# A decoder of two blocks on one core: the filler products taken out of the norms and of the routing

## What is computed

```python
for l in range(DEPTH):                      # first block
    h = rms_norm(x, g_pre[l]) * (1.0 + scale) + shift
    ...                                     # projections, three attentions, gates -> y
    x = x + gate * rms_norm(y, g_post[l])
...
hn = rms_norm_2(h, norm_mix[0]); h = h + even_mixer(hn, ...)
h = h + swiglu(rms_norm_2(h, norm_ffn[0]), ...)
hn = rms_norm_2(h, norm_mix[1]); h = h + odd_mixer(hn, ...)
h = h + moe_swiglu(rms_norm_2(h, norm_ffn[1]), router, w1, w3, w2)
return rms_norm_2(h, norm_final)

logits = t @ router                         # inside moe_swiglu
top_vals, top_idx = lax.top_k(logits, 2)
top_w = softmax(top_vals)
```

## Time and profile before

| | |
|---|---|
| median of three timed runs | 1960.36 us (1958.73 to 1962.9) |
| the profiled execution | 1962.08 us |
| its span, first to last instruction | 1958.8 us |
| mean granted clock of TensorE | 0.988 |
| busy share of the span: PE, PE's weight loads, DVE, ACT | 98%, 80%, 61%, 49% |
| chain that ended last: PE, DMA, DVE, ACT | 62%, 2%, 1%, 1% |

### The profile page before, as it was taken

The page is one execution under the profiler, slowest core; times in us unless marked ns, Lnnn a source line. Parts: engine busy times, 40 slices in busy tenths (PEclk is TensorE's granted clock), DMA queues, the critical chain, the costliest instruction groups (busy, mean ns, idle before and its releaser), DMA issues.

```text
span 1958.8 us, 30650 instructions
## 1 busy us (share of the span) xinstructions
PE 1918.3 (98%) x12361; PEld 1570.0 (80%) x12361; DVE 1185.5 (61%) x1698; ACT 969.5 (49%) x1429; POOL 29.8 (2%) x29
## 2 busy tenths in 40 slices
PE   6999999999999999999999999999999999999998
PEld 4999899999899989999999736883588887368833
DVE  4767886565785776666663217951498884059611
ACT  3647753466863575443463206740476673057501
POOL 1000000000000120000000000000000000000000
PEclk7999999999999999999999999999999999999999
DMA  9985556465544542555455899999999999999997
GB/s 291 270 267 184 163 174 160 98 188 189 158 140 140 177 142 88 194 194 158 158 187 203 336 395 407 416 365 412 409 413 409 404 374 347 414 408 411 409 410 303
DMA packets 292565, 536.83 MB, mean 274 GB/s; under 512 B 67076, under 2 KB 198600, under 8 KB 278096
## 3 DMA queue, kind: packets, MB, share of 16 engines
q1 hardware_dynamic: 287968, 530.82, 75.4%
q10 hardware_dynamic: 3920, 3.69, 0.6%
q0 software_dynamic: 544, 0.43, 0.1%
HBM read 533.83 MB, written 1.07 MB: 273 GB/s over the span
## 4 chain that ended last, share of the span: by engine, by line
PE 62%; DMA 2%; DVE 1%; ACT 1%; issue 0%; SPq 0%; DVEq 0%
PE bank L803 14%; PE bank L805 14%; PE bank L804 13%; PE bank L1603 9%; PE bank L1630 4%; DMA pool<-in_od_exp_w 2%; PE bank L1411 1%; PE bank L1458 1%; PE bank L1487 1%; PE bank L1519 1%; PE bank L763 1%; PE bank L748 1%; PE bank L1616 0%; PE bank L788 0%; PE bank L779 0%
## 5 line engine op out<-in xcount | busy, mean ns | idle before, releaser
L3123 DVE TENSOR_TENSOR expert_lo<-pool,w_hi 128x2048 fp32r<-128x2048 f32 x168 | 376.9, 2287 | 46.6 <-ACT w_hi L2268 46.5
L2268 ACT ACTIVATE w_hi<-pool 128x2048 fp32r<-128x2048 f32 x168 | 313.2, 1912 | 29.4 <-DMA pool<-in_od_exp_w 25.3
L803 PE MATMUL bank<-h_upper,upper 128*128 128x256 f32 x1056 | 310.0, 294 | 2.1 <-DVE ring_lo L2537 2.0
L804 PE MATMUL bank<-h_lo,upper 128*128 128x256 f32 x1056 | 300.5, 285 | 0.0
L805 PE MATMUL bank<-h_upper,ring_lo 128*128 128x256 f32 x1056 | 300.4, 284 | 0.0
L2537 DVE TENSOR_TENSOR ring_lo<-ring,upper 128x1024 fp32r<-128x1024 f32 x148 | 179.7, 1222 | 102.9 <-ACT upper L1785 102.6
L803 PEld LDWEIGHTS bank<-h_upper,upper 128*128 128x128 f32 x1056 | 204.1, 193 | 9.6 <-issue 8.5
L804 PEld LDWEIGHTS bank<-h_lo,upper 128*128 128x128 f32 x1056 | 204.3, 193 | 1.0 <-issue 0.4
L805 PEld LDWEIGHTS bank<-h_upper,ring_lo 128*128 128x128 f32 x1056 | 204.1, 193 | 0.0
L1603 PE MATMUL bank<-pool,xe_light 128*64 128x512 f32 (+1 forms) x976 | 187.4, 539 | 2.8 <-issue 2.0
L2847 DVE TENSOR_TENSOR piece_lo<-ring,piece_hi 128x1024 fp32r<-128x1024 f32 x118 | 144.7, 1237 | 73.9 <-ACT piece_hi L1774 73.6
(11 more groups left out here) (482 smaller groups left out, 3605.0 us busy)
## 6 DMA issues: line engine op xcount, KB each, us to landing
pool<-in_od_exp_w SPq DMA_DIRECT2D x330, 1024.0 KB, 13.9
ring<-in_w_in SPq DMA_DIRECT2D x48, 1024.0 KB, 5.7
ring<-in_ev_ffn_w SPq DMA_DIRECT2D x33, 1024.0 KB, 5.3
ring<-in_w_ada SPq DMA_DIRECT2D x24, 1024.0 KB, 7.7
ring<-in_od_w_in SPq DMA_DIRECT2D x12, 1024.0 KB, 5.4
ring<-in_ev_w_in SPq DMA_DIRECT2D x10, 1024.0 KB, 5.4
ring<-in_w_in SPq DMA_DIRECT2D x32, 256.0 KB, 4.5
ring<-in_w_out SPq DMA_DIRECT2D x8, 1024.0 KB, 4.9
```

What stands on the lines that cost most here:

```text
L803: nc.tensor.matmul(b, left[0], right[0], start=first, stop=False, skip_group_check=True)
L804: nc.tensor.matmul(b, left[0], right[1], start=False, stop=False, skip_group_check=True)
L2268: nc.scalar.activation(w_hi[q % HIS], ring_slot(q), ACT.Copy)\
L3123: V.tensor_tensor(low_slot(q), ring_slot(q), w_hi[q % HIS].bitcast(F32), ALU.subtract)\
```

## The change

The function `keep_busy` and all its calls are taken out. The order of all other work, on every engine, stays as it was.

```diff
-        def keep_busy(n):
-
-            b = order["attn"][turn["attn"] % 4]
-            pe.wait_ge(*busy[b])
-            for _ in range(n):
-                nc.tensor.matmul(bank[b][:, 0:P], mean[1024], ident, start=True, stop=True)
-
...
                 token_squares(("pre", l))
-                keep_busy(4)
                 spread(("pre", l), 0, NT, h_ready, "pre", l, KD - 1)
-                keep_busy(6)
             project(*((("cq", l, j), proj_ready, (("cq", l), j)) for j in range(2)), fresh=("pre", l))
...
                 mean_square_part(("post", l), c, "attn")
-            keep_busy(4)
             spread(("post", l), 0, NT, dve_step, "yo", l, KD - 2)
-            keep_busy(12)
...
         token_squares(("mix", 0))
-        keep_busy(4)
         spread(("mix", 0), 0, NT, h_ready, "mix", 0, KD - 1)
-        keep_busy(5)
         pe.wait_ge(flog_spread, when(flog_spread, "all"))
...
         token_squares(("mix", 1))
-        keep_busy(6)
         spread(("mix", 1), 0, NT, h_ready, "mix", 1, KD - 1)
-        keep_busy(6)
         w = take("lr")
...
-        keep_busy(3)
         pe.wait_ge(loaded_moe, when(loaded_moe, "all"))
...
         m.then_inc(psum_ready, wrote("pos"))
-        keep_busy(4)
```

## The result

The changed kernel took 1974.24 us (1971.68 to 1976.01), the kernel before in the same comparison 1960.25: ratio 1.0068, interval 1.0055 to 1.0082, some 13 to 14 us slower. The forecast was slower, 1965.4, in a range of 1961.0 to 1970.0: the sign was right, the size nearly three times too small.

A forecast was written before the change was run, and what follows sets the result against it. The prediction took PE, with 62% of the chain, to set the end. Its terms 1.0 + 1.7 - 0.1 + 2.4 summed to +5.0 us on the 1960.36 median, giving 1965.4 us, range 1961.0 to 1970.0.

The forecast's parts named there:

- What bounds the kernel: Whole kernel: PE, with 62% of the chain, sets the end; its delays come out in full where nothing else is late.
- How long the low clock lasts: Where dense products must bring the clock back: 4.4 us low, losing 1.9 us; ends 3.3 and 6.8 us.
- The longest low stretch anywhere is 6.8 us: Reading of the granted clock in the profile before, used as the upper end for a low stretch.
- First norm: Post of layer 0, pre of layer 1, 26 fillers: spread 0.95 us earlier, projection loses 1.9; +1.0 us (+0.5 to +2.0).
- they stay so, at no cost: First norm's squares: already slow at 5.54 us, they would remain so without fillers and add nothing.
- Second norm: Post of layer 1, mix 0, 25 fillers: slower squares, forget logits 0.2 us earlier but losing 1.9; +1.7 us (+1.2 to +2.8).
- Third norm: Mix 1, 12 fillers: low-rank product some 2.0 us earlier, then loses 1.9 at low clock; -0.1 us (-0.6 to +1.0).
- Routing: 7 fillers delaying nothing: clock falls without them, 5.5 us low into the experts' first products; +2.4 us (nothing to 3.0).
- The price: 256-column products start 0.213 us apart at 1.2 GHz, 0.120 at 2.4; a low stretch T loses 0.44 T.
- Much slower: Rival: clock falls in each place for 6.8 us or twice; +8.8 up to +12, about 1970.5 us; chance 0.15.
- The fillers only stand in the way: Rival: clock returns at once or doesn't fall, so only blocked work comes back; -2.2, 1958.1 us; chance 0.13.

The follow-up runs named there:

- +4.4 alone: Only the 26 fillers of the first norm taken out of the kernel before: 1963.66 us against 1959.25, ratio 1.0023.
- +3.0 (0.6 to 4.5 by the ratio's ends) alone: Only the 25 fillers of the second norm taken out of the kernel before: 1962.29 us against 1959.25, ratio 1.0013.
- +0.4 alone: Only the 12 fillers of the third norm taken out of the kernel before: 1960.64 us against 1960.23, ratio 1.0001.
- 3.5 to 4.3 alone: Only the 7 fillers of the routing taken out of the kernel before: 1962.73 us against 1959.25, ratio 1.0022.
- one-column run: Kernel before with all 70 fillers kept, each streaming one moving column instead of 128: 1977.87 us against 1959.25, ratio 1.0091.
- wide kernel: Kernel before with all fillers, the width-1024 norms' squares products streaming 128 columns instead of one: 1956.6 us against 1959.33, ratio 0.9987.

## Why the prediction was right or wrong

**What bounds the kernel** was right: PE's chain passed the delays on, the single places adding up at the end.

**How long the low clock lasts** is the step that failed. I took 4.4 us (5.5 in the routing), from two stretches that dense work ended, and 6.8 as the longest. But that prices only the end of a stretch. Without fillers the fall comes before the sparse work, at 338.0 and 645.2 us in the first two norms and at 1109.4 us in the routing, and all that follows up to the dense products is done at 1.2 GHz: 20.3, 16.7, 6.7 and 13.5 us, of which only the last part has dense work. The traces add 13.3 us where the sum had 5.0; 3.5 of the difference lie in the routing, 2.3 in the first norm, 2.2 in the second. "The longest low stretch anywhere is 6.8 us" was a misreading: the start's is 20.5 us in the profile of before, and I used its last 5.5 us only.

**First norm**, +1.0 forecast, +3.3 in the traces and +4.4 alone. What the spread gives back was there: it starts 1.2 us earlier behind its reciprocal, not 0.95 (PE starts 0.04 us after VectorE's result, not 0.25), and 1.0 of it reaches the scaling of h. Wrong was "they stay so, at no cost": the 5.54 us of the squares were a mean, begun at the high clock, and all at the low one they take 6.96, 1.4 more. The sum had no term for the post norm's spread, which takes 1.22 us instead of 0.61 and so sets VectorE back by 0.4. And in the profile of before the clock came back under the last six fillers, at 352.3; without them the projection ran low from its start at 352.96 until 358.5 us, which costs it 2.4 us, not 1.9. With the 1.0 given back this makes the 3.3.

**Second norm**, +1.7 forecast, +3.9 in the traces and +3.0 (0.6 to 4.5 by the ratio's ends) alone: the mechanism was right and both terms too small. The squares took 6.96 us, not 5.54, so that the reciprocal came 1.2 us later in its frame than I had it; the forget logits lost 3.0 us, not 1.9.

**Third norm**, -0.1 forecast, +0.2 in the traces, +0.4 alone (within its noise): right, with its two terms. The low-rank product starts 2.1 us earlier behind the last square and takes 2.3 longer.

**Routing**, +2.4 forecast, +5.9 in the traces, 3.5 to 4.3 alone: the mechanism was right and the size not. The gathers alone lose 3.3 us and the first experts' products 2.6, at 13.5 us of low clock instead of 5.5. The text took all seven fillers as the cover; it is the four behind the position products.

**The price**, 0.44 us for each us at the low clock, is right for dense products (the projection's steps are 0.213 us apart in the low part of the changed kernel: 355.23 to 355.87 for three). Over whole stretches and all kernels it is 0.31, as part of a stretch is waiting for other engines (in the first row of the changed kernel PE is busy for 14.86 of 20.30 us).

**The rivals.** "Much slower" came nearest, with 6.8 us or two such stretches a place, and stopped at +12; it was given 0.15. "The fillers only stand in the way" was wrong for the time as a whole, and its rule, that idle gaps alone count, fell with the one-column run. (At the fall of 649.3 us, which the prediction lays to one-column squares, the squares had ended at 648.54 and fillers ran; a gap there was not, as it says. Its "first block's end" and "second's" are the ends of the first block's two layers.)

## What to carry to other kernels

A product that nobody reads can be worth more than it costs: read the granted clock of the stretch before taking it out, and price the loss by the whole stretch from the last dense products to the next, not by how fast dense work brings the clock back. Look also for columns where the work is: here the squares' products streamed 128 columns instead of one for 0.1 us in 32 products, and with the fillers in place the clock then stayed at 2.4 GHz through all three norms, with nothing more standing in front of real work. If the time at the low clock can be read from every run's mean clock, plot it against the span before looking for other causes.

## What the runs showed that I had not expected

PE without a gap stood at 1.2 GHz for 23.5 us on end, 18 of them in one-column products and two spreads: its busy share does not tell the clock. The same 32 records take 6.96 us at one level and 3.63 at the other, 0.2175 against 0.113 us each; so products of one column, each with its own weight load, lose at the low clock at least as large a share as the 256-column products, 0.213 against 0.120. With 128 columns streamed, the squares of the first norm take 4.36 us in the wide kernel, all at the high clock; with one column they took 5.54, in part at the low one, and those of the second norm 4.25, at the high one. Where the clock falls by chance differs between executions of one kernel: the stretch at the start was 13.7 to 20.5 us long in the profiles of kernels that share it, and the low time of the 87 timed runs of before goes from 27 to 51 us, with a correlation of 0.75 to their spans, which lie between 1952.2 and 1962.2.
